# A delta-rule core moved into the recurrence's block, with another order of groups and pieces

## The reference

```python
# gated delta rule: 8 heads of 128, in chunks (the kernel takes chunks of 128 tokens as units: 6)
lmat = where(strict, (k * beta) @ k.T * decay, 0)
tmat = inverse(eye + lmat)                       # triangular
v_new = tmat @ (v * beta) - (tmat @ (kb * exp(g))) @ state
o = q_head @ state + attn @ v_new
state = state * exp(g_last) + k_tail.T @ v_new
# rwkv: 16 heads of 64, one step for each token
state = state * w + (-(state @ kk)) * b + v * k
o = state @ r
```

## Time and profile before

| | us |
|---|---|
| median of 3 runs | 3907.0 |
| lowest and highest | 3905.72 and 3909.22 |
| the profiled execution: its own time | 3900.54 |
| the profiled execution: its span | 3898.8 |
| its mean granted clock of PE | 0.944 |
| PE busy | 3410.6 (87%) |
| DVE busy | 2173.3 (56%) |
| ACT busy | 1104.0 (28%) |
| POOL busy | 782.8 (20%) |

### The profile page before, as it was taken

One profiled execution on the slowest core, in us unless ns is written; L12 is line 12 of the kernel. 1 busy time (PEld: TensorE's weight loads), 2 busy tenths in 40 slices (PEclk: granted clock), 3 DMA queues, 4 the chain that ended last, 5 costly groups with the idle time before them and its releaser, 6 DMA issues. The chain is left out here.

```text
span 3898.8 us, 50924 instructions
## 1 busy us (share of the span) xinstructions
PE 3410.6 (87%) x19656; PEld 2854.0 (73%) x19656; DVE 2173.3 (56%) x4083; ACT 1104.0 (28%) x1776; POOL 782.8 (20%) x644
## 2 busy tenths in 40 slices
PE   8679999989999588788888877889798999999897
PEld 1168888868888488788877767888576777787485
DVE  2543565655555456666666664687402188886323
ACT  1214454543333122221222121232102234431202
POOL 0000000000000111221212210000375443446174
PEclk9889999999999899999999996899899999999998
DMA  9122343444555434454544532433342322222232
GB/s 384 44 74 91 127 137 128 136 130 164 155 188 168 121 89 112 118 138 104 127 108 114 129 101 83 127 117 105 146 136 70 129 77 82 81 77 81 78 117 74
DMA packets 337341, 464.71 MB, mean 119 GB/s; under 512 B 189856, under 2 KB 236032, under 8 KB 330608
## 3 DMA queue, kind: packets, MB, share of 16 engines
q1 hardware_dynamic: 272576, 364.28, 30.1%
q0 software_dynamic: 26512, 83.08, 7.4%
q10 hardware_dynamic: 38048, 14.56, 1.6%
HBM read 382.80 MB, written 81.63 MB: 119 GB/s over the span
## 5 line engine op out<-in xcount | busy, mean ns | idle before, releaser
L1007 PE MATMUL pjl<-high,w_high 128*128 128x512 f32 x816 | 326.9, 401 | 22.9 <-DVE low L2562 16.3
L1009 PE MATMUL pjl<-high,w_low 128*128 128x512 f32 x816 | 319.6, 392 | 0.0
L1008 PE MATMUL pjl<-low,w_high 128*128 128x512 f32 x816 | 319.5, 391 | 0.0
L1992 POOL DMA_DIRECT2D arena_r<-in_w_ada x256 | 138.4, 541 | 787.1 <-DVE arena_r L2341 737.6
L2992 DVE SCALAR_TENSOR_TENSOR arena<-arena,par 128x512 f32<-128x512 f32 x232 | 250.1, 1078 | 6.9
L1139 DVE TENSOR_TENSOR wl_in<-ring,wh_in 128x1024 fp32r<-128x1024 f32 x136 | 164.2, 1221 | 136.1 <-ACT wh_in L1132 136.1
L990 POOL TENSOR_TENSOR w_low<-ring_o,w_high 128x1024 fp32r<-128x1024 f32 x88 | 221.4, 2516 | 6.9
L1120 PE MATMUL pjl<-h_high,wh_in 128*128 128x512 f32 x544 | 214.6, 394 | 9.2 <-DVE wl_in L1139 9.2
L1981 POOL MEMSET unused<- 128x1 f32 x3 | 0.2, 99 | 1103.0 <-POOLq L197 1103.0
L1120 PE MATMUL xu<-h_high,wh_in 128*128 128x512 f32 x544 | 220.4, 405 | 0.0
L2632 POOL TENSOR_TENSOR w_low<-ring_o,w_high 128x1024 fp32r<-128x1024 f32 x64 | 169.7, 2652 | 252.6 <-ACT w_high L2821 251.9
(11 more groups left out here) (478 smaller groups left out, 8192.0 us busy)
## 6 DMA issues: line engine op xcount, KB each, us to landing
ring<-in_w_lr SPq DMA_DIRECT2D x136, 512.0 KB, 4.2
arena_r<-in_w_ada POOLq DMA_DIRECT2D x256, 256.0 KB, 3.2
arena<-in_w_ada SPq DMA_DIRECT2D x32, 1024.0 KB, 11.1
ring_o<-in_w_out SPq DMA_DIRECT2D x64, 512.0 KB, 3.7
ring_o<-in_w SPq DMA_DIRECT2D x64, 512.0 KB, 3.6
arena_r<-rk_d SPq DMA_DIRECT2D x94, 192.0 KB, 5.3
rk_d<-arena_p SPq DMA_DIRECT2D x72, 192.0 KB, 1.9
arena_p<-gate_rows SPq DMA_DIRECT2D x32, 386.0 KB, 6.3
```

The costliest lines, as they stand in the source:

```text
L1007: pe.matmul(lat, wh[:, c], ah, start=kk == 0, stop=False)
L1008: pe.matmul(lat, wh[:, c], al, start=False, stop=False)
L1009: last = pe.matmul(lat, wl[:, c], ah, start=False, stop=kk == KT - 1)
L1992: pool.dma_start(late[:, x % LATE], io["w_ada"][8 + x // 16, :, x % 16]).then_inc(S[f"r_lw{x % LATE}"], 16)
```

## The change

1. `phase_gdn` becomes `delta_core`, which returns four functions, one for each engine's stream, and `phase_rwkv` calls them in its own block. The block's end and its barrier between the two are gone. The delta core's tiles lie over tiles of the recurrence that are dead by then; the scan's first set, the state and the output buffers lie over `heads_out`'s.
2. In the last pair's second half `fill1` runs `start(0, n)`. `rest` runs `start(1, n)`, `invert(0, n)`, the last `heads_out` and, four in each of pieces 2 to 17, the modulation columns. `load_c(0)` waits for the recurrence's last output to be stored (`r_y`, `r_st`).
3. The groups go BT, CT, LC, MB, MC, CV, one to a piece up to piece 8. The elimination steps lie in pieces 5, 6 and 7 (4, 5 and 6 steps). In piece 5 they go ahead of the group. The loads of the next K, B and C blocks wait for MC instead of CT.
4. In steps 2 and 3 DVE runs `fill(3*j)` after it has copied SA and scaled the state. `LATER` is spread anew.
5. In phase two the gates' products 0 to 3 stand between shorter pieces of the convolution.

```diff
-            sp.dma_start(bmask, io["base16"]).then_inc(S["g_b16"], 16)
+        sp.wait_ge(S["r_q"], 16 * PAIRS)
         load_a(0)
-            load_b(0)
-            load_c(0)
         hops(0)
         load_a(1)
+        sp.wait_ge(S["r_oa"], 1 + 16 * PAIRS)
+        load_b(0)
         hops(1)
         load_a(2)
+        sp.wait_ge(S["r_y"], 1 + PAIRS)
+        sp.wait_ge(S["r_st"], 1 + 16 * PAIRS)
+        load_c(0)
         load_b(1)
...
+        def rest(heads_out):
+
             for n in range(18):
                 start(1, n)
                 invert(0, n)
+                if n == OUT_AT:
+                    heads_out()
+                if 1 < n:
+                    if n == 2:
+                        pe.wait_ge(S["r_lu"], 256)
+                    for q in range(4 * n - 8, 4 * n - 4):
+                        last = pe.matmul(shares[:, q:q + 1], acc[:, q // 4, q % 4 * P:q % 4 * P + P], ones[:, 0:1], start=True, stop=True)
+            last.then_inc(S["g_sh"], 1)
...
+        def rest(heads_out):

             dve.memset(eps[:], 1e-6).then_inc(S["g_v0"], 1)
-            dve.memset(LB, 0.0).then_inc(S["g_v0"], 1)
-            dve.wait_ge(S["g_v0"], 2)
-            dve.wait_ge(S["g_b16"], 16)
             for n in range(18):
-                start(0, n)
-            for n in range(18):
+                if n in OUT_DVE:
+                    heads_out(OUT_DVE.index(n))
                 invert(0, n) if n < 3 else None
                 start(1, n)
                 invert(0, n) if n >= 3 else None
+            dve.wait_ge(S["r_st"], 1 + 16 * PAIRS)
             start(2, 0)
...
-LATER = {0: 1, 2: 1, 8: 1, 9: 1, 11: 1, 13: 2, 14: 2, 15: 1, 16: 3, 17: 3}
-R_GROUPS = {1: (0,), 2: (1,), 3: (2, 3), 4: (4, 5), 5: (6,), 6: (7,), 7: (8,), 8: (9,), 9: (10, 11), 10: ()}
-R_STEPS = {5: range(0, 4), 6: range(4, 7), 7: range(7, 11), 8: range(11, 15)}
-R_TURNED, R_DONE, R_BACK = 5, 8, 10
+LATER = {1: 2, 2: 2, 4: 1, 8: 2, 11: 1, 13: 2, 14: 2, 16: 2, 17: 2}
+R_GROUPS = {n: range(n - 1, n) for n in range(1, 9)} | {9: range(8, 10), 10: range(10, 12)}
+R_STEPS = {5: range(0, 4), 6: range(4, 9), 7: range(9, 15)}
+R_TURNED, R_DONE, R_BACK = 5, 7, 9
...
-    GROUPS = [(name, d) for name in ("LC", "MB", "MC", "BT", "CT", "CV") for d in range(2)]
+    GROUPS = [(name, d) for name in ("BT", "CT", "LC", "MB", "MC", "CV") for d in range(2)]
...
-                sp.wait_ge(S["r_p"], i * 12 + 12)
+                sp.wait_ge(S["r_q"], i * 16 + 14)
                 load_a(i + 1, 0)
...
                 def fill1(n):
                     if more:
                         prepare(i * 2 + 2, 0, n)
+                    else:
+                        delta_start(0, n)
...
-            heads_out(PAIRS - 1)
+            delta_rest(lambda: heads_out(PAIRS - 1))
...
-                    fill(3 * j)
+                    if j not in (2, 3):
+                        fill(3 * j)
                     later(i, hh, 3 * j)
...
                     link(last)
+                    if j in (2, 3):
+                        fill(3 * j)
                     fill(3 * j + 1)
...
-            conv(7, 4, 14)
             product(0)
-            conv(7, 14, 23)
+            conv(7, 4, 9)
             product(1)
-            conv(7, 23, 31)
-            for k in range(2, 8):
+            conv(7, 9, 14)
+            product(2)
+            conv(7, 14, 20)
+            product(3)
+            conv(7, 20, 31)
+            for k in range(4, 8):
                 product(k)
...
-PHASES = [(phase_mod, "a"), (phase_gates, "b"), (phase_proj, "pq"), (phase_rwkv, "r"), (phase_gdn, "g"),
+PHASES = [(phase_mod, "a"), (phase_gates, "b"), (phase_proj, "pq"), (phase_rwkv, "rg"),
           (phase_out, "o"), (phase_two, "nz")]
```

More of the change, by code:

```diff
@@ new lines, in start @@
+                    for u in range(UN):
+                        last = pe.matmul(tp[:, d, u], k_a[:, u * P:u * P + P], KB[:, d, u * P:u * P + P], start=True, stop=True)
+                    last.then_inc(S["g_lt"], 1)
+            elif n == 2:
+                pe.wait_ge(S["g_ltc"], 2 * a + 2)
+                for u in range(4):
+                    last = pe.matmul(tp[:, 0, u], k_a[:, u * P:u * P + P], q_a[:, u * P:u * P + P], start=True, stop=True)
+                last.then_inc(S["g_mt"], 1)
@@ L729, in scan @@
-                    fill(m, 3 * j + 2)
-            for n in range(18):
-                start(0, n)
-            for q in range(64):
-                last = pe.matmul(shares[:, q:q + 1], acc[:, q // 4, q % 4 * P:q % 4 * P + P], ones[:, 0:1], start=True, stop=True)
-            last.then_inc(S["g_sh"], 1)
+                        pe.matmul(o_[:, d], old[:, d], QG[m % 2][:, d, u * P:u * P + P], start=True, stop=False)
+                        last = pe.matmul(o_[:, d], SA[:, d], MT[m % 3][:, d, u], start=False, stop=True)
@@ L796, in _ @@
             for n in range(18):
-                start(0, n)
-            for n in range(18):
+                if n in OUT_ACT:
+                    heads_out(OUT_ACT.index(n))
                 start(1, n)
                 invert(0, n)
+            act.wait_ge(S["r_st"], 1 + 16 * PAIRS)
             start(2, 0)
@@ L1921, in phase_rwkv @@
     W, SA, St, Sn = carve(2, 64), carve(2, 64), carve(2, 64), carve(2, 64)
+    late = carve(LATE, 512)
+    at_kept = e["at"][0]
+    Z = carve(2, UN, 16)
+    LBr, LB, ZBr, ZB, tm = (carve(256) for _ in range(5))
+    bmask = carve(8)
     rp = carve(R_NPAR)
@@ L1924, in phase_rwkv @@
     eps = carve(1)
-    late = carve(LATE, 512)
+    arena, unit = e["arena"], 2 * UN * P
+    free = dict(Z=Z, LBr=LBr, LB=LB, ZBr=ZBr, ZB=ZB, tm=tm, bmask=bmask, soon=arena[:, 0:3 * unit], G=arena[:, 3 * unit:4 * unit],
+                LT=arena[:, 4 * unit:5 * unit], ET=arena[:, 5 * unit:6 * unit], then=arena[:, at_set:at_out], last=arena[:, at_out:at_kept])
+    delta_sync, delta_tensor, delta_scalar, delta_vector = delta_core(nc, e, free)
     csk, acc = e["csk"], e["arena"][:, CORE - 16 * 512:].rearrange("p (g c) -> p g c", c=512)
@@ L2423, in _ @@
             pair(PAIRS - 1, False)
-            for n in range(4):
-                heads_out(PAIRS - 1, n)
+            delta_rest(lambda n: heads_out(PAIRS - 1, n))
 def phase_out(nc, e):
```

698 lines of the change are left out of this document (355 added, 343 removed).

## The result

The changed kernel takes 3883.8 us (median of 4 runs, 3881.75 to 3885.53), the kernel before beside it 3906.69 us: ratio 0.9943, 95% interval 0.9931 to 0.9955, 22.9 us less. Measured once more among the experiments it was 3887.29 against 3901.99 us, ratio 0.9958 (0.9944 to 0.9972). Forecast were 3866 us, with a range of 3800 to 3905. So the sign and the range held; of the 41 us expected, some 15 to 23 came.

A forecast was written before the change was run, and what follows sets the result against it. TensorE was taken as the engine everything is built around, with waits in recurrence, seam and gates. 3900.5 minus 36 (seam), plus 6 (recurrence, opening), minus 11 (gates) is 3859.5; with 6.5 for the median, 3866 us, range 3800 to 3905.

The forecast's parts named there:

- the likeliest case: The whole kernel at the forecast of 3866 us, chance 0.47, own range 3845 to 3890 us.
- Gates, minus 11: Phase two: products moved ahead of convolution pieces remove PE's 9.17 us wait and the half-rate matmuls behind it, minus 11 us.
- DVE's convolutions end as before, 30 us ahead of the last product: Phase two's gates: moving the products leaves the end of DVE's convolution work unchanged, 30 us before the last product.
- The rival with GpSimd in it: Phase two: the gates' stall stays because GpSimd's splits set the pace once PE no longer waits; 3877 us, chance 0.07.
- Seam, minus 36: From the recurrence's last half to the scan: first delta copy at about 111 us instead of 146.8, minus 36 us.
- "12 us" for the output and the table switches: In the seam: DVE's centring and two ACT table switches add 12 us between head 1's keys and the first merge.
- 12 for the columns and the output: In the seam, from merge to end of inverse: 12 us of share columns and output transposes lie on the path.
- Rival three: The seam gives back 20 us through a late set and late adds in the crowded half; 3886 us, chance 0.13.
- Table switches: ACT in the joined stretch: the skill's drain, some 4 us less gain over three switches, was not counted.
- Recurrence, plus 0.6 a pair: Recurrence: one half plus 4.4 us, the other minus 3.8, so plus 0.6 a pair, plus 5 us over 7.5 pairs.
- The first rival: The recurrence gains too: waits on load, inverse and memset go unreplaced; 3791 us, partly 3830, chance 0.20.
- The opening: The recurrence stage's opening: the mask now waits for CV, plus 1 us.

The follow-up runs named there:

- the differences first: The changed kernel with head 1's decay differences ahead of the last output's centring and head 0's mask on DVE: 3881.3 us, ratio 0.9944.
- 48 columns: The changed kernel with 48 of the 64 modulation columns left out, so its result is incomplete: 3881.76 us, ratio 0.9945.
- the last of the sums: The changed kernel with fifth gates' product among convolution pieces, old recurrence order, head 1's differences first, and scan's first set loaded before head 2's keys: 3870.17 us.
- the fifth product: The changed kernel with the fifth gates' product (number 4) also put among the convolution pieces: 3878.42 us, ratio 0.9932.

## Why the prediction was right, and where it was off

- **Sign, range, chances.** Held; the likeliest case's own range, 3845 to 3890, too. The median was missed by 18 us. Of the profiled execution's own time, 3859.5 expected and 3884.5 measured, 12 us are the gates, 7 the seam, 3 the recurrence with its opening, and 3 are stages that the change doesn't touch.
- **Gates, minus 11: wrong.** The failed step is "DVE's convolutions end as before, 30 us ahead of the last product" and the spacing built on it. It took durations from a stretch in which PE's stall had kept GpSimd still; measured, DVE's convolution ends 85 us after the first gates' tile begins, not 62, and 17 us ahead of the last product. The rival with GpSimd in it, 3877 us, had the size but not the cause: GpSimd's pace did not set PE's; its instructions hold up DVE's. The products alone gave 1.0004, and one product more 10 us.
- **Seam, minus 36: 29 measured.** Its landmarks came true to 2 us as far as head 1's keys. The step mis-sized was "12 us" for the output and the table switches between the keys and the first merge, 16 measured (2359.3 to 2375.4), as DVE came to head 1's differences 5.4 us after the keys, which their own rows account for only in part: with the differences first it still came to them 3.8 us after the keys. From the first merge to the first product of values and keys (L674, now L692) it was 38.0 us, 13.1 more than the 24.9 of before, where the forecast had 12 for the columns and the output: as sized. But what counts for the scan is the store, and there it was 29.2 us behind the merge, not 26. At equal clock 48 columns reach it with only 2.1 us; the 24 matmuls at the lower clock, 2.3 us longer, are most of what was missed, and no term had this stretch's clock. Rival three (a seam that gives back 20 us) did not come.
- **Table switches.** ScalarE: Activation LUTs in the Trainium skill, "What ACT_TABLE_LOAD costs", adds a drain to each load. The traces speak against it here as the earlier trace rows did: in that of the last of the sums the activation ahead ends at 2421.96, the load at 2421.98 lasts 1.28 us, and the next activation starts at 2423.28, 0.02 us behind it.
- **Recurrence, plus 0.6 a pair: 0.6 in the two profiled executions,** 1.0 in the mean of all traces. By steps the working held in part: first steps minus 3.9 (minus 2.7), step 2 plus 4.9 (plus 5.3), step 3 plus 4.5 (plus 2.6), steps 4 and 5 minus 2.5 (minus 0.8); second half minus 4.1, plus 5.7, minus 0.1, minus 3.8 (minus 4.5, plus 4.8, minus 1.9, minus 2.2). The sum was right by luck, through errors that cancel: the early and late steps gained more, and step 3 lost what they gained. One term does not follow from its own parts: four evictions (3.8) against three late adds (2.3) are minus 1.5, not minus 2.7. What is missing in the working is the diff's own fourth point: no term for the evictions of MC queued behind DVE's copy of SA. It costs 5.1 us a pair (4.2 in step 3 of the first half), and the recurrence's other edits gain 4.3; with a price on it the reader would have seen that this one edit takes back what they bring. The first rival's mechanism shows in part once it is undone (3848 us against its 3830 for the case in part): the waits on load, inverses and memset stay small, while those on the state update are 49.7 us, not the 25.4 of before.
- **The opening** costs 3 us, not 1 (59.5 us in the changed kernel's traces, 56.7 before).

## What to carry to other kernels

A wait on an in-order engine costs what is queued behind it: before a block of work is moved behind a copy that waits for another engine, look whether that other engine will soon need the block's results. Take an operation's duration from a stretch in which the other engines do what they will do after the change, since a stall elsewhere may be what makes it fast. And take a change with several edits apart on the chip even when it is a gain: here one edit took back 37 us by the traces (33 by the times) of the 59 that the others had brought, 30 in the pairs and 29 in the seam.

Not run: the kernel with the old fill calls together with the fifth product and the differences first. From 3848, less 10 and up to 5, an estimate is 3833 to 3838 us.

## What had not been expected of the hardware

- A DVE instruction with two inputs in SBUF (128x512, fp32) takes 0.76 us alone and 2.26 to 2.89 us when it meets a GpSimd instruction of 1.9 to 2.9 us, which it waits out.
- A store of two times 48 KB issued 0.4 us behind a load of 1542 KB landed later: 6.45 us to the next step instead of 2.06, though their data have nothing to do with each other.
- The set's load took 13.0 us behind head 2's keys and gate rows, and 6.5 us with nothing but that store beside it.
